# First stage: the last panel's batches ahead of two granules, four raw tiles for gMLP's weights, two modulation batches in flight, and edits around the last retention panel and the end

## What is computed

```python
for l in range(2):
    mod = silu(c) @ w_mod[l] + b_mod[l]                  # shift, scale, gate: 3 x 2048 for each of 9 streams
    h = rms_norm(x, norm_g[l]) * (1 + scale) + shift
    if l == 0:                                           # u, va, za (gMLP); q, k, vb, zb (retention, 8 heads)
        proj = h @ w_in_e                                # 2048 x 14336
        ya = gelu(u) * spatial_gating(layer_norm(gelu(va))) * silu(za)   # 4 heads, 512 wide
        yb = rms_norm(retention(rotary(q), rotary(k), vb, state)) * silu(zb)
        y = concat([ya, yb]) @ w_out_e                   # 4096 x 2048
    else:                                                # gated linear attention, 8 heads
        y = gla(h @ w_in_o, state) @ w_out_o
    x = x + gate * y
return rms_norm(x, final_g), new states, va rows
```

## Time and profile before

| what | us |
|---|---|
| median of three runs | 2802.64 (2798.71 to 2806.12) |
| the profiled execution | 2805.92 |
| its span, first to last instruction | 2804.3 |
| TensorE busy in the span | 2725.0 |
| first stage: start to granule 8 | 143.13 |
| last matmul's end to the end of the span | 19.5 |

### The profile page before, as it was taken

How to read it: one execution, slowest core, us unless ns; L and a number is a source line. 1 busy time by engine, 2 the same in 40 slices (tenths; PEclk the granted TensorE clock), 3 DMA queues, 4 the chain that set the end, 5 groups by cost and what they waited for, 6 DMA issues and landing times. The chain is left out here.

```text
span 2804.3 us, 36959 instructions
## 1 busy us (share of the span) xinstructions
PE 2725.0 (97%) x13345; PEld 2072.5 (74%) x13345; DVE 1260.8 (45%) x1834; ACT 884.8 (32%) x1237; POOL 540.7 (19%) x631
## 2 busy tenths in 40 slices
PE   6899999999999999999988999999999999999997
PEld 3567777777788888888877867787768777787865
DVE  2234343333345555455544454544544464544544
ACT  1323222222233332223322534332434334422421
POOL 2101021001301112211123120231122121231123
PEclk8999999999999999999999999999999999999998
DMA  9677676666744555455444364655556364655453
GB/s 364 252 238 264 210 249 228 212 213 226 231 132 161 169 173 192 141 174 171 161 146 132 93 217 129 224 157 177 160 180 193 116 231 147 200 149 187 151 188 128
DMA packets 296656, 523.35 MB, mean 187 GB/s; under 512 B 26601, under 2 KB 125049, under 8 KB 295609
## 3 DMA queue, kind: packets, MB, share of 16 engines
q1 hardware_dynamic: 256450, 389.17, 43.0%
q0 software_dynamic: 40064, 132.31, 14.0%
HBM read 460.40 MB, written 60.96 MB: 186 GB/s over the span
## 5 line engine op out<-in xcount | busy, mean ns | idle before, releaser
L1535 PE MATMUL acc<-whi,hT_hi 128*128 128x512 f32 x2496 | 998.6, 400 | 6.1 <-ACT work L829 3.2
L1535 PE MATMUL acc<-whi,hT_lo 128*128 128x512 f32 x2496 | 975.5, 391 | 0.0
L1535 PE MATMUL acc<-wlo,hT_hi 128*128 128x512 f32 x2496 | 975.2, 391 | 0.0
L1047 DVE TENSOR_TENSOR wlo<-raw,whi 128x1024 fp32r<-128x1024 f32 x413 | 518.2, 1265 | 611.9 <-ACT whi L723 610.1
L723 ACT ACTIVATE whi<-raw 128x1024 fp32r<-128x1024 f32 x413 | 435.6, 1059 | 929.0 <-PE acc L1535 929.0
L1535 PEld LDWEIGHTS acc<-whi,hT_hi 128*128 128x128 f32 x2496 | 470.5, 188 | 175.9 <-issue 74.4
L1535 PEld LDWEIGHTS acc<-whi,hT_lo 128*128 128x128 f32 x2496 | 470.2, 188 | 101.1
L1535 PEld LDWEIGHTS acc<-wlo,hT_hi 128*128 128x128 f32 x2496 | 470.9, 189 | 91.2
L1058 DVE TENSOR_TENSOR wlo<-raw,whi 128x1024 fp32r<-128x1024 f32 x131 | 165.6, 1265 | 330.6 <-ACT whi L737 329.7
L1535 PE MATMUL acc<-whi,yT_hi 128*128 128x512 f32 x768 | 303.4, 395 | 1.3 <-DVE yT_lo L1172 1.2
L1535 PE MATMUL acc<-wlo,yT_hi 128*128 128x512 f32 x768 | 300.0, 391 | 0.0
(11 more groups left out here) (216 smaller groups left out, 1817.9 us busy)
## 6 DMA issues: line engine op xcount, KB each, us to landing
raw<-in_w_in_o SPq DMA_DIRECT2D x384, 256.0 KB, 3.1
raw<-in_w_in_e SPq DMA_DIRECT2D x256, 256.0 KB, 3.0
state<-in_w_mod SPq DMA_DIRECT2D x112, 512.0 KB, 5.9
raw<-in_w_in_e SPq DMA_DIRECT2D x96, 512.0 KB, 4.4
out<-state POOLq DMA_DIRECT2D x96, 512.0 KB, 3.3
state<-in_state_gla POOLq DMA_DIRECT2D x64, 512.0 KB, 5.1
raw<-in_w_out_o SPq DMA_DIRECT2D x128, 256.0 KB, 3.4
raw<-in_w_mod SPq DMA_DIRECT2D x56, 512.0 KB, 5.9
```

Of the source, the lines that this page charges most:

```text
L1047: dve.tensor_tensor(wlo[jj][:, :, :], raw[jj][:, :, :], whi[jj][:, :, :].bitcast(F32), ALU.subtract).then_inc(s["lo_ready"], 1)
L1535: return pe.matmul(out, lhsT, rhs, start=start, stop=stop, skip_group_check=True)
```

## The change

1. First stage: panel 7's four batches run without a granule between them; granule 4 follows after the last batch and granule 5 between the turns of the input. ACT copies panels 2, 4 and 6 out before it splits the granule that stood in front of that copy.
2. gMLP's granules from n = 8 on have all four raw tiles; the later batches of `w_mod` have slots 1 and 2 alone, so two in flight. SP's waits change with that.
3. Retention: all four state tiles are read first (`ret_read`), then come the updates in two rounds (`ret_round`); DVE normalises earlier; POOL takes the root first and multiplies by the gate between the second and the third store. The last head is written out of its loop.
4. Last retention panel: the normalising comes before the updates, the second round follows the fourth granule, turning no longer waits for all updates, and the first gate rows have a tile of their own and are issued by POOL ahead of the last two stores.
5. End: `final_g` is loaded during the last panel, DVE adds the last third of `x` itself, and products and stores are done in halves of 1024 columns.

```diff
-SLOT = [nb % 5 if nb < 8 * NBATCH else (nb - 30) % 3 for nb in range(N_MOD * NBATCH)]
+SLOT = [nb % 5 if nb < 8 * NBATCH else 1 + nb % 2 for nb in range(N_MOD * NBATCH)]
...
+        fin_g = carve(2580, D)
...
-        out_g = {"gm": carve(6656, 2, W), "rt": carve(5776, 2, W), "gl": carve(7444, 2, W)}
+        out_g = {"gm": carve(6656, 2, W), "rt": carve(5776, 2, W), "last rt": carve(4752, 2, W), "gl": carve(7444, 2, W)}
...
-        main_in = [sem(f"main_in{k}") for k in range(2)]
+        main_in = [sem(f"main_in{k}") for k in range(NSLOT)]
...
+        def main_slot(n):
+            return n - N_GM if n >= N_GM else (1, 3, 0, 2)[n % 4] if n >= 8 else 2 * (n % 2)
         def main_raw(n):
-            return raw[n - N_GM if n >= N_GM else 2 * (n % 2)][:, :, :]
+            return raw[main_slot(n)][:, :, :]
+        def main_turn(n):
+            return sum(main_slot(m) == main_slot(n) for m in range(n + 1))
...
-                with eng.Fori(0, 3) as hh:
+                with eng.Fori(0, 3 - ph) as hh:
                     ret_head(ph, hh + 1, ("rt", ph * 4 + hh, ph * 8 + hh * 2 + Y_RT, hh * 2))
+            ret_head(1, 3, ("rt", 6, 12 + Y_RT, 4))
...
-                    if j % 2:
-                        sp.wait_ge(s["mod_used"], N_MOD * NBATCH - 2)
-                    else:
-                        sp.wait_ge(s["lo_ready"], N_GM - 1 + j // 2)
+                    sp.wait_ge(s["lo_ready"], N_GM - 3 + (2, 0, 3, 1)[j])
...
-                at_least(sp, s["lo_ready"], n - 1)
-                sp.dma_start(raw[2 * (n % 2)][:, :, :], src).then_inc(main_in[n % 2], 16)
+                if n in (8, 9):
+                    sp.wait_ge(s["mod_used"], max(nb for nb in range(8 * NBATCH) if SLOT[nb] == 0) + 1)
+                else:
+                    at_least(sp, s["lo_ready"], n - 1 if n < 8 else n - 3)
+                sp.dma_start(main_raw(n), src).then_inc(main_in[main_slot(n)], 16)
...
-                    sp.wait_ge(s["final_done"], t + 1)
                     dst = y_s.rearrange("b l d -> (b l) d") if t == 2 else y_p[0, P * t:P * t + P, :]
-                    sp.dma_start(dst, x[:, t, :]).then_inc(s["y_out"], 16)
-                sp.wait_ge(s["y_out"], 16 * NT)
+                    for c in range(2):
+                        sp.wait_ge(s["final_done"], 2 * t + c + 1)
+                        sp.dma_start(dst[:, D // 2 * c:D // 2 * c + D // 2], x[:, t, D // 2 * c:D // 2 * c + D // 2])\
+                            .then_inc(s["y_out"], 16)
+                sp.wait_ge(s["y_out"], 32 * NT)
...
+                if not (kind == "rt" and before and not behind):
+                    gate_rows(out_g["last rt" if kind == "rt" and not behind else kind])
+                if last:
+                    pool.wait_ge(s["pst_out"], 16 * (B_HEADS + C_HEADS))
+                    pool.dma_start(fin_g, a["final_g"].partition_broadcast(P)).then_inc(s["fg_in"], 16)
+                for t in range(2 if last else NT):
...
-                for c in range(CH_RT):
+                rsqrt(h + (2 + A_HEADS))
+                for c in range(2):
                     st_store(ret_piece, ret_s[0], h, c, h * CH_RT + c, 4)
-                rsqrt(h + (2 + A_HEADS))
                 pool.wait_ge(s["o_done"], h * NT + NT + LEAD)
                 products(ai + 2, onb, lambda t: wb[:, t, :])
+                if isinstance(h, int) and h == B_HEADS - 1:
+                    pool.wait_ge(s["yb_full"], Y_RT + 2 * YB)
+                    g = out_g["last rt"]
+                    pool.dma_start(g[:, 0, :], gate_dram[0, 0, 0:W].partition_broadcast(P)).then_inc(s["g_in"], 16)
+                    pool.dma_start(g[:, 1, :], gate_dram[0, 1:NC9, 0:W]
+                                   .rearrange("b (o n) -> b o n", o=1).to_broadcast([NB, LS, W])).then_inc(s["g_in"], 16)
+                for c in range(2, CH_RT):
+                    st_store(ret_piece, ret_s[0], h, c, h * CH_RT + c, 4)
                 st_free(h + 1)
...
-                pool.wait_ge(s["x_added"], NT * 32 + LEAD)
-                apart(pool)
-                pool.dma_start(work[:, 0:D], a["final_g"].partition_broadcast(P)).then_inc(s["fg_in"], 16)
...
-                for m in range(8):
-                    if m:
-                        panel_out(m - 1)
-                    if m < 2:
-                        continue
+                panel_out(0)
+                for m in range(2, 8):
                     k0 = 4 * (m // 2 - 1)
                     if m % 2 == 0:
+                        panel_out(m - 1)
                         act.wait_ge(s["sel_done"], m)
                         for k in (k0, k0 + 1, k0 + 2):
                             prompt(0, k)
...
                             act.activation(wsT_all[:, :, m // 2 - 2, :],
                                            OB[0][:, :].rearrange("p (h t) -> p h t", h=A_HEADS),
                                            ACT.Copy).then_inc(s["wsT_done"], 1)
+                        panel_out(m)
                         split_main(m - 2)
...
                     if kind == "rt" and before:
+                        ret_norm(before)
                         ret_update(before, 0)
                         ret_update(before, 1)
                     split(r, 1)
-                    if kind == "rt" and before:
-                        ret_update(before, 2)
-                        ret_update(before, 3)
-                        ret_norm(before)
                     if kind != "rt" and before:
                         turned(before, 0, True)
                         turned(before, 2, True)
...
                     if kind == "rt" and before:
                         turned(before, 0, True)
                     split(r, 3)
-                panel_done(kind, ai, oi, r, 3)
+                panel_done(kind, ai, oi, r, 3, None if behind or kind != "rt" else "last rt")
+                if kind == "rt" and before:
+                    ret_update(before, 2)
+                    ret_update(before, 3)
...
                 split(r, 2)
+                if before:
+                    ret_norm(before)
                 split(r, 3)
                 if before:
                     ret_update(before, 2)
                     ret_update(before, 3)
                 split(r + 1, 0)
-                if before:
-                    ret_norm(before)
...
-                dve.wait_ge(s["x_added"], NT * 32 + LEAD)
+                dve.drain()
+                xs = x[:, 2, 3 * W:4 * W]
+                dve.tensor_tensor(xs, xs, out_tmp["gl"][:, 2, :], ALU.add)
+                dve.drain()
+                dve.wait_ge(s["x_added"], NT * 32 - 1 + LEAD)
                 x_stats(3)
                 norm(4, None, 2 + A_HEADS + B_HEADS + C_HEADS)
                 dve.wait_ge(s["fg_in"], 16)
                 for t in range(NT):
-                    dve.scalar_tensor_tensor(out=x[:, t, :], in0=x[:, t, :], scalar=rstd[:, t:t + 1],
-                                             in1=work[:, 0:D], op0=ALU.mult, op1=ALU.mult).then_inc(s["final_done"], 1)
+                    for c in range(2):
+                        part = x[:, t, D // 2 * c:D // 2 * c + D // 2]
+                        dve.scalar_tensor_tensor(out=part, in0=part, scalar=rstd[:, t:t + 1],
+                                                 in1=fin_g[:, D // 2 * c:D // 2 * c + D // 2],
+                                                 op0=ALU.mult, op1=ALU.mult).then_inc(s["final_done"], 1)
...
-                            va_main(m - 3)
-                        if m % 2 and b == 2:
-                            va_main(m - 2)
+                        if m in (3, 5) and b in (0, 2):
+                            va_main(m - 3 + b // 2)
...
+                va_main(4)
                 select(7, OB[0])
-                for k in range(12, KT):
-                    turn_x(0, k)
+                turn_x(0, 12)
+                turn_x(0, 13)
+                va_main(5)
+                turn_x(0, 14)
+                turn_x(0, 15)
...
-                        pe.wait_ge(s["up_done"], h * (2 * CH_RT) + 2 * CH_RT)
+                        pe.wait_ge(s["up_done"], h * (2 * CH_RT) + (CH_RT if wide else 2 * CH_RT))
...
                             ret_prompt(before)
-                            ret_pieces(before, 0)
-                        if g == 1:
-                            ret_pieces(before, 2)
+                            ret_read(before)
+                            ret_round(before, 0)
                         if g == 2:
                             turn_out(before, 0, True)
                             turned(before)
+                        if g == 3:
+                            ret_round(before, 2)
...
+            def ret_read(before):
+                h = before[1]
+                for c in range(CH_RT):
+                    pe.wait_ge(st_in[c], h * 16 + 16)
+                for kt in range(KH):
+                    for b in (0, 2, 4, 6, 1, 3, 5, 7):
+                        g0, half = 32 * (b // 2), DVB * (b % 4)
```

(35 more changed lines are left out.)

## The result

The changed kernel takes 2810.3 us (median of 16 runs, 2808.1 to 2814.4) against 2803.0 (16 runs, 2797.3 to 2807.3): ratio 1.003, 95% interval 1.0022 to 1.0038, so slower by 0.3%, where 2788 was forecast. The first stage and the end gained about what was forecast, the last retention panel more. What the prediction priced at 0.5 under "Two batches in flight" costs 25.

What follows compares the result with a forecast made beforehand. TensorE, busy 2725 of 2804.3 us, was taken as the bound. Gains 11.5 + 2.5 + 0.9 - 0.5 = 14.4 took the profiled 2805.92 to 2791.5; the median, 3.28 lower, gave 2788, range 2780 to 2797.

Steps and rivals of the forecast that it cites:

- The first stage: First stage: earlier copies out, new granule order, no gelu wait and its clock loss; 10.6 to 12.3 us gained, taken as 11.5.
- the end: After the last matmul: earlier statistics, no wait for final_g, smaller last store; 2.5 us gained, bounds 1.7 and 3.
- the last retention panel: Last retention panel: earlier normalising and turn, less a later stall; 0.9 us gained, bounds 4.6 and -1.
- Two batches in flight: Batches wait longer and SP holds granules behind them; cost 0 to 1.5 us at three places, taken as +0.5.
- The step that failed: In the 52 single batches, granules are issued 17.5 us before needed and need 9.5, so nothing is late.
- The double panel: Head 0's third projection, the tightest place: spare time between 2.5 and -0.1 us after the change.
- SP's queue: Rival, chance 0.05: waiting batches hold granules past their time, all 52 single batches pay; at 0.5 us each, 2814.
- 8 us spare: Argument against the slower rival: granules in the single batches are issued 17.5 us ahead and need 9.5.
- that floor: First stage: transfers keep the last batch from landing before 107.1 us, whatever TensorE does.
- The estimate of 98: First stage: the last batch's landing floor if transfers ran at the ports' some 435 GB/s.
- The clock holds: Rival, chance 0.20: TensorE's clock stays up after the first stage's shorter copy waits; some 4 us more, 2784.
- the second stall: Second panel after the last retention panel's turn: late stores delay POOL's add and gate rows; TensorE stalls 3 us.

Runs made afterwards that it cites:

- part 2 alone: The kernel before the change with only part 2 of the change added; 2823.7 us, ratio 1.0075.
- without part 2: The changed kernel with part 2 undone (three batches in flight, two raw tiles, SP's waits as before); 2789.4 us, ratio 0.9952.
- batch behind next pair: The changed kernel, but SP issues each batch of the later panels behind the next pair of granules; 2784.9 us, ratio 0.9939.
- products first: The changed kernel, but in gMLP's output panels DVE makes the products ahead of the last of four splits; 2795.8 us, ratio 0.9977.

## Why the prediction was wrong

Measured terms: first stage -11.2 (orders 6.1, gelu 3.4, clock behind it 1.7), retention loops -0.6, last retention panel -3.4, end -2.8, part 2 behind the stage +25.2. The sum is +7.2; the medians differ by 7.3. So close a fit is partly luck, for the stage's term rests on traces that scatter.

**The step that failed** is "the granules issue four granules and a batch before they are needed (17.5) and need 6.9 + 2.6 = 9.5; nothing is late". The need was nearly right: from SP's release at 353.26 to ACT's start at 363.36 it is 10.1, of which 8.5 are the load from its issue, and to DVE's split at 364.45 it is 11.2. The deadline was wrong. I measured to TensorE's use of the granule, but its split stands three granules ahead in the programs of ACT and DVE, and whatever is queued behind it falls due first. In an output panel a pair is released when TensorE starts the panel's second pair, and the products behind its split are due when that pair ends: 9.4 us (two granules and a batch), not 17.5. Need 11.2, the rest of the split 1.15 and the first product 0.83: 13.2 against 9.4 is 3.8 short, and TensorE waits 3.85. In the single panels of the heads ACT's gelu stands behind the splits of the next pair only, which is released two pairs before it is due (18.7): nothing lost there.

**The double panel**, taken at +0.5 with bounds 0 to 1.5, lost 9.5 to 11.9. I weighed only the low part's lateness, and its wait is indeed 0.48; the copy, tanh and silu behind the splits cost 4.00 and 2.95 more, and clock.

**The rival "SP's queue"** named the mechanism and got 0.05, with the wrong place: 52 batches at 0.3 to 0.5 each. It decides at seven output panels and one projection, and that its 2814 lies near the 2810.3 measured is luck. The argument against it ("8 us spare") was the failed step again.

**The first stage** came out as forecast, 11.2 against 11.5, and nearly by the forecast's parts: the orders 6.1 (forecast 9 to 11 less the gelu's 3.2, so 6 to 8), the gelu 3.4, the clock 1.7 (1.5). The 11.2 leans on "part 2 alone" for the stage before; the two profiled traces by themselves differ by 16.65, because the forecast started from a long one. The last batch was forecast to land at 109.4, and not before 107.1 whatever TensorE does; in after it is used at 106.47 without a wait, so that floor did not hold. The estimate of 98 beside it scales the whole time from the span's start; over 60 to 111, which the rows cover, the same scaling gives about 102. "The clock holds" is right in part: select now runs in 1.03. In after the clock still falls behind it (0.52 in 103 to 106) and is back by granule 4; in three of the five traces with both orders and four tiles it does not fall there, and granule 8 starts at 128.1 to 129.5 in these, at 128.2 and 130.8 in the two others, so the 4 us that a held clock was to give do not show.

**Last retention panel.** The first steps hold with the 7.9 that after is late there: the normalising at 1430.9 (forecast 1431.3), the turn at 1443.1 (1443.4), the second stall at 2.33 (3), and moving the stores shows its cause. The term was too small (-0.9): up to granule 280 it is -1.9, as the clock stays up at the second stall in this trace, and 1.5 more come at the start of the next layer, which I had not followed. **The end:** 2.5 forecast, 2.8 measured. Part 3: nothing forecast, 0.6 gained.

## What to carry to other kernels

When a load is issued later, compare its landing with the time at which its first reader stands in that engine's program, and then with the due time of everything queued behind that reader; the consumer's own deadline can be slack and still say nothing. Put a transfer that waits for a buffer behind those that can go at once: here that one exchange on SP turned +0.3% into -0.6%, and the stores behind the adds made it -0.7%. Before a term is read off two traces, look where runs of one kernel differ among themselves; here it is the first stage, by nearly 5 us.

## What the runs showed of the hardware

A wait of 3.85 us before granule 52 cost 6.6: behind it TensorE ran at 1.2 GHz (0.50, where 1.00 is 2.4 GHz) until about 372. Nearly the same wait before granule 116, 3.84, cost 5.5, with a shorter stretch at half (0.50 in 693 to 696).

The length of a wait alone does not tell whether the clock falls. Windows behind two pairs of like waits at the same place of the program, columns as in the windows above. Before granule 280, 2.44 in "without part 2" and 2.44 in "batch behind next pair":

```profile
1464.00:1467.00 3.00, 3.00 (x9) 2.31 (x8) 1.31 (x1) 0.00 (x0) 3.00 (x3) 0.50 0.80 258
...
1457.00:1460.00 3.00, 3.00 (x15) 2.47 (x14) 1.57 (x2) 0.00 (x0) 3.00 (x3) 1.00 0.89 289
```

Before granule 24, 2.99 in "products first"; the other of this pair is the 2.95 in after, whose window of 220 to 222 stands above (1.00):

```profile
221.00:224.00 3.00, 3.00 (x8) 2.32 (x8) 0.75 (x2) 0.40 (x1) 3.00 (x3) 0.50 1.05 399
```

What decides between 0.50 and 1.00 there stays open. The Trainium skill (TensorE: Matmul & The Clock Gate, "HAM oscillation") says that long waits between bursts re-throttle the engine; 3.85 bears it out, and 2.44 shows that a shorter wait can do it too.

The transfers of the first stage ran at 395 GB/s for 44 us on end in after, where the kernel before had 355 in its trace. The change is not needed for that: "part 2 alone", with the first stage's orders of before, had 392 in 60 to 104.
